# A hybrid attention and recurrence layer: values stationary in the heads, probabilities turned by a product with a diagonal of reciprocals, the branch's gate turned by VectorE and DMAs

## What is computed

```python
qh = _rms(heads(q)) * q_norm_w
kh = _rms(heads(k)) * k_norm_w
vh = heads(v)
log_f = log_sigmoid(f_logit + b_f)          # F = cumsum(log_f) over the sequence
# per head: s[t, u] = q_t . k_u / sqrt(128) + F_t - F_u for u <= t, p = softmax(s), att = p @ v
att = _forgetting_attention(qh, kh, vh, log_f)
y_a = att * silu(z_a)
y_a = einsum('bsw,wd->bsd', y_a, w_br_attn)
```

## Time and profile before

| | us |
|---|---|
| median of 3 runs | 2555.03 |
| lowest, highest | 2553.88, 2555.07 |
| the profiled execution's own time | 2555.0 |
| its span in the trace | 2553.2 |
| TensorE busy | 2522.7 (99%) |
| VectorE busy | 2013.0 (79%) |
| ScalarE busy | 1445.9 (57%) |
| GpSimd busy | 319.3 (13%) |

### The profile page before, as it was taken

The page is one execution under the profiler, slowest core; times in us unless marked ns, Lnnn a source line. Parts: engine busy times, 40 slices in busy tenths (PEclk is TensorE's granted clock), DMA queues, the critical chain, the costliest instruction groups (busy, mean ns, idle before and its releaser), DMA issues.

```text
span 2553.2 us, 31860 instructions
## 1 busy us (share of the span) xinstructions
PE 2522.7 (99%) x11399; PEld 2092.8 (82%) x11399; DVE 2013.0 (79%) x2163; ACT 1445.9 (57%) x1719; POOL 319.3 (13%) x577
## 2 busy tenths in 40 slices
PE   6999999999999999999999999999999999999999
PEld 5888888888888888888888888888888888888887
DVE  6999999999887666775777777668787878788885
ACT  6787666655555465655666666543434443555553
POOL 0000000000000000224556655200000000000000
PEclk9999999999999999999999999999999999999999
DMA  9999999999999666557777777789998989676675
GB/s 351 361 330 344 354 362 355 381 364 351 367 347 298 175 195 187 162 159 200 208 210 211 208 210 214 205 309 371 344 348 311 349 312 349 221 229 200 199 230 165
DMA packets 389617, 705.11 MB, mean 276 GB/s; under 512 B 36194, under 2 KB 99924, under 8 KB 388948
## 3 DMA queue, kind: packets, MB, share of 16 engines
q1 hardware_dynamic: 370656, 695.05, 81.5%
q0 software_dynamic: 18288, 7.90, 1.6%
q10 hardware_dynamic: 516, 0.13, 0.0%
HBM read 694.55 MB, written 7.88 MB: 275 GB/s over the span
## 4 chain that ended last, share of the span: by engine, by line
PE 96%; DMA 1%; SPq 1%; DVE 1%; ACT 0%; issue 0%; DVEq 0%; ACTq 0%
PE ps_acc L1650 27%; PE ps_acc L1585 25%; PE ps_acc L1587 25%; PE ps_t L1585 3%; PE ps_t L1587 3%; PE ps_t L1650 3%; PE ps_acc L1601 2%; PE ps_acc L1603 2%; SPq L624 1%; PE ps_acc L1642 0%; PE ps_acc L1644 0%; PE ps_acc L1643 0%; DMA land<-in_w_out 0%; DMA land<-in_w_gate 0%; PE ps_t L1725 0%; PE ps_t L1642 0%
## 5 line engine op out<-in xcount | busy, mean ns | idle before, releaser
L739 ACT ACTIVATE w_hi<-land 128x1024 fp32r<-128x1024 f32 x860 | 909.7, 1059 | 935.9 <-PE ps_acc L1587 588.0
L1019 DVE TENSOR_TENSOR w_lo<-land,w_hi 128x1024 fp32r<-128x1024 f32 x860 | 1049.8, 1222 | 399.9 <-ACT w_hi L739 394.1
L1585 PE MATMUL ps_acc<-w_hi,h_hi 128*128 128x512 f32 x2324 | 907.3, 390 | 0.5 <-ACT w_hi L739 0.5
L1587 PE MATMUL ps_acc<-w_hi,h_lo 128*128 128x512 f32 x2324 | 904.7, 389 | 0.0
L1650 PE MATMUL ps_acc<-w_lo,h_hi 128*128 128x512 f32 x2564 | 685.7, 389 | 1.1 <-DVE w_lo L1019 1.1
L1650 PEld LDWEIGHTS ps_acc<-w_lo,h_hi 128*128 128x128 f32 x2564 | 481.1, 188 | 101.9 <-DVE w_lo L1019 2.1
L1585 PEld LDWEIGHTS ps_acc<-w_hi,h_hi 128*128 128x128 f32 x2324 | 436.3, 188 | 91.6 <-ACT w_hi L739 1.3
L1587 PEld LDWEIGHTS ps_acc<-w_hi,h_lo 128*128 128x128 f32 x2324 | 436.5, 188 | 89.5
L1028 DVE SCALAR_TENSOR_TENSOR acc<-ada_ring,cvec,acc 128x1024 f32<-128x1024 f32 (+1 forms) x291 | 300.5, 1033 | 17.6 <-DMA ada_ring<-in_w_ada 10.9
L603 POOL DMA_DIRECT2D store<-xz x512 | 272.4, 542 | 198.1 <-DVE xz L1372 158.9
L1428 DVE SCALAR_TENSOR_TENSOR racc<-res_land,cvec,racc 128x1024 f32<-128x1024 f32 x124 | 158.7, 1280 | 0.9 <-DMA res_land<-in_w_ada 0.9
(11 more groups left out here) (304 smaller groups left out, 2339.2 us busy)
## 6 DMA issues: line engine op xcount, KB each, us to landing
land<-in_w_in SPq DMA_DIRECT2D x384, 512.0 KB, 5.5
land<-in_w_gate SPq DMA_DIRECT2D x256, 512.0 KB, 4.8
ada_ring<-in_w_ada SPq DMA_DIRECT2D x160, 512.0 KB, 6.2
res_land<-in_w_ada SPq DMA_DIRECT2D x128, 512.0 KB, 7.7
land<-in_w_out SPq DMA_DIRECT2D x92, 512.0 KB, 4.5
ada_ring<-in_w_ada SPq DMA_DIRECT2D x140, 256.0 KB, 5.0
land<-in_w_br_attn SPq DMA_DIRECT2D x64, 512.0 KB, 4.6
land<-in_w_br_rnn SPq DMA_DIRECT2D x64, 512.0 KB, 5.9
```

The costliest lines, as they stand in the source:

```text
L739: act.activation(w_hi[:, n % PARTS], land[:, n % LAND], ACT.Copy).then_inc(hi_rdy, 1)
L1019: dve.tensor_tensor(w_lo[:, n % PARTS], land[:, n % LAND], w_hi[:, n % PARTS].bitcast(F32), ALU.subtract).then_inc(split_done, 1)
L1585: pe.matmul(sums[:, t], l_hi(kk, t), w_hi[:, n % PARTS, kk], start=first and kk == 0 and not added, stop=False, skip_group_check=added)
L1587: ins = pe.matmul(sums[:, t], l_lo(kk, t), w_hi[:, n % PARTS, kk], start=False, stop=False, skip_group_check=added)
```

## The change

Four things change together.

1. The value step has v stationary and `prt` moving, so its result `ps_o` has channels on partitions as the next projection wants it. The step "y" on TensorE, its two transposes and its PSUM tile go; ScalarE rounds and VectorE splits straight from `yt` in SBUF.
2. The softmax's reciprocals are then needed along the free dimension. VectorE makes, per head, two diagonal matrices `diag` from `ident` and the reciprocals (`head_scale`), right behind the exponentials in the same slot, and TensorE's `probs` step is three full products of `pr` with `diag` in place of three transposes: it turns and scales at once.
3. The gate `z_a` must be multiplied in channels on partitions, too. `turn_za`, behind units 315, 319, ... 343 on VectorE, turns two heads at a time into the single buffer `za_turned`; GpSimd issues 16 DMAs per turning (128 in all) that write it back to `store`, between its `f_diff` of head 0 and of head 1. Each `turn_za` after the first waits until the DMAs of the one before have landed (`za_in`). Head 0's `prt` waits for all of them.
4. The order of steps within a slot: ScalarE has "y" ahead of "score", VectorE has "score", "y", "value" and then `head_scale`.

```diff
-PE_ORDER = ("score", "value", "y", "probs", "turn")
-ACT_ORDER = ("turn", "probs", "score", "y")
-DVE_ORDER = ("score", "probs", "value", "y")
+PE_ORDER = ("score", "value", "probs", "turn")
+ACT_ORDER = ("turn", "probs", "y", "score")
+DVE_ORDER = ("score", "y", "value")
...
+ZA_AT = {N_F + 28 + 4 * g: g for g in range(HEADS // 2)}
...
+        za_turned = at("za_turned", [P, BPJ, 2, NT, 32], F32, r_scr + 6 * K)
+        diag = [at(f"diag{h}", [P, NT, P], F32, blk(K_BLK + h)) for h in range(HEADS)]
...
             for h in range(HEADS):
+                if h == 1:
+                    for g in range(HEADS // 2):
+                        pool.wait_ge(za_t, g + 1)
+                        for i in range(BPJ):
+                            for jj in range(BPJ):
+                                pool.dma_start(store[32 * jj:32 * jj + 32, ZA_BLK + 2 * g:ZA_BLK + 2 * g + 2, :,
+                                                     32 * i:32 * i + 32].rearrange("p b t d -> p (b t) d"),
+                                               za_turned[32 * i:32 * i + 32, jj].rearrange("p b t d -> p (b t) d")
+                                               ).then_inc(za_in, 16)
                 pool.wait_ge(f_row_in[h % 2], h // 2 * 16 + 16)
...
+                    else:
+                        act.wait_ge(za_in, HEADS // 2 * 16 * BPJ * BPJ)
                     act.activation(prt[:], ps_p, ACT.Copy).then_inc(prt_rdy, 1)
                 if step == "y":
-                    act.wait_ge(y_t, h + 1)
-                    if h < HEADS - 1:
-                        act.wait_ge(y_rdy, 2 * h + 4)
-                    act.activation(ya_hi[:, h], ps_y, ACT.Copy).then_inc(ya_h, 1)
+                    act.wait_ge(y_rdy, h + 1)
+                    act.activation(ya_hi[:, h], yt[:], ACT.Copy).then_inc(ya_h, 1)
...
-                if step == "probs":
-                    dve.wait_ge(pr_rdy, 2 * h + 2)
-                    dve.reciprocal(rden[:, h % 2], den[:, h % 2]).then_inc(rden_rdy, 1)
                 if step == "value":
-                    dve.wait_ge(rden_rdy, h + 1)
                     dve.wait_ge(valued, h + 1)
                     if h:
-                        dve.wait_ge(y_t, h)
-                    for t in range(NT):
-                        dve.scalar_tensor_tensor(yt[:, t], ps_o[:, t], rden[:, h % 2, t:t + 1], store[:, ZA_BLK + h, t],
-                                                 ALU.mult, ALU.mult).then_inc(y_rdy, 1)
+                        dve.wait_ge(ya_rdy, h)
+                    dve.wait_ge(za_in, HEADS // 2 * 16 * BPJ * BPJ)
+                    dve.tensor_tensor(yt[:], ps_o, store[:, ZA_BLK + h], ALU.mult).then_inc(y_rdy, 1)
...
+            def head_scale(h):
+                dve.wait_ge(pr_rdy, 2 * h + 2)
+                st.did(dve.reciprocal(rden[:, h % 2], den[:, h % 2]))
+                st.sync()
+                for t in range(NT):
+                    dve.tensor_scalar(diag[h][:, t], ident[:], rden[:, h % 2, t:t + 1], None, ALU.mult
+                                      ).then_inc(diag_rdy, 1)
+
+            def turn_za(g):
+                dve.wait_ge(f_kept, 16)
+                dve.wait_ge(acc_free, FREED[FINAL["za", 3]][1])
+                if g:
+                    dve.wait_ge(za_in, g * 16 * BPJ * BPJ)
+                for i in range(2):
+                    ins = dve.transpose(za_turned[:, :, i].rearrange("p j t b -> p t j b"),
+                                        store[:, ZA_BLK + 2 * g + i].rearrange("p t (j a) -> p t j a", j=BPJ))
+                    if i == 0:
+                        st.did(ins)
+                ins.then_inc(za_t, 1)
...
+                if "score" in HEADS_AT.get(n - 2, {}):
+                    head_scale(HEADS_AT[n - 2]["score"])
+                if n in ZA_AT:
+                    turn_za(ZA_AT[n])
...
-                    for k in range(3):
-                        ins = pe.transpose(ps_p[:, k], pr[:, k], ident[:])
+                    pe.wait_ge(diag_rdy, NT * (h + 1))
+                    for k, t in enumerate((0, 1, 1)):
+                        ins = pe.matmul(ps_p[:, k], pr[:, k], diag[h][:, t], start=True, stop=True)
                     ins.then_inc(pr_t, 1)
...
-                    pe.matmul(ps_o[:, 0], prt[:, 0], store[:, V_BLK + h, 0], start=True, stop=True)
-                    pe.matmul(ps_o[:, 1], prt[:, 1], store[:, V_BLK + h, 0], start=True, stop=False)
-                    pe.matmul(ps_o[:, 1], prt[:, 2], store[:, V_BLK + h, 1], start=False, stop=True
+                    pe.matmul(ps_o[:, 0], store[:, V_BLK + h, 0], prt[:, 0], start=True, stop=True)
+                    pe.matmul(ps_o[:, 1], store[:, V_BLK + h, 0], prt[:, 1], start=True, stop=False)
+                    pe.matmul(ps_o[:, 1], store[:, V_BLK + h, 1], prt[:, 2], start=False, stop=True
                               ).then_inc(valued, 1)
-                if step == "y":
-                    pe.wait_ge(y_rdy, h * 2 + 2)
-                    if h:
-                        pe.wait_ge(ya_rdy, h)
-                    for t in range(NT):
-                        ins = pe.transpose(ps_y[:, t], yt[:, t], ident[:])
-                    ins.then_inc(y_t, 1)
```

More of the change, by code:

```diff
@@ L308 @@
 assert RG_START[-1] + RG_EVERY + 10 <= N_R + 5
+ZA_AT = {N_F + 28 + 4 * g: g for g in range(HEADS // 2)}
+assert N_F + 28 + 4 * (HEADS // 2 - 1) < N_HEAD
 MT_AT = {N_O - RU + 1 + 2 * k: k for k in range(CH)}
@@ L483, in build @@
         ps_o = ps_d[:, 0:2 * P].rearrange("p (a b) -> p a b", a=2)
-        ps_y = ps_d[:, 2 * P:4 * P].rearrange("p (a b) -> p a b", a=2)
         seq = lambda b: store[:, b].rearrange("p t d -> p (t d)")
@@ L522, in build @@
                                                  sem("pr_t"), sem("prt_rdy"))
-        valued, rden_rdy, y_rdy, y_t, ya_h, ya_rdy = (sem("valued"), sem("rden_rdy"), sem("y_rdy"), sem("y_t"), sem("ya_h"),
-                                            sem("ya_rdy"))
+        valued, diag_rdy, y_rdy, ya_h, ya_rdy = sem("valued"), sem("diag_rdy"), sem("y_rdy"), sem("ya_h"), sem("ya_rdy")
+        za_t, za_in = sem("za_t"), sem("za_in")
         bias_in, gate_rdy, gate_used = sem("bias_in"), sem("gate_rdy"), sem("gate_used")
@@ L1349, in head_step @@
                     dve.tensor_reduce(mx[:, 1:2], ps_s[:, 1:3], AX.XY, ALU.max, negate=True).then_inc(mx_rdy, 1)
-                if step == "probs":
-                    dve.wait_ge(pr_rdy, 2 * h + 2)
-                    dve.reciprocal(rden[:, h % 2], den[:, h % 2]).then_inc(rden_rdy, 1)
                 if step == "value":
-                    dve.wait_ge(rden_rdy, h + 1)
                     dve.wait_ge(valued, h + 1)
                     if h:
-                        dve.wait_ge(y_t, h)
-                    for t in range(NT):
-                        dve.scalar_tensor_tensor(yt[:, t], ps_o[:, t], rden[:, h % 2, t:t + 1], store[:, ZA_BLK + h, t],
-                                                 ALU.mult, ALU.mult).then_inc(y_rdy, 1)
+                        dve.wait_ge(ya_rdy, h)
+                    dve.wait_ge(za_in, HEADS // 2 * 16 * BPJ * BPJ)
+                    dve.tensor_tensor(yt[:], ps_o, store[:, ZA_BLK + h], ALU.mult).then_inc(y_rdy, 1)
                 if step == "y":
                     dve.wait_ge(ya_h, h + 1)
-                    dve.tensor_tensor(ya_lo[:, h], ps_y, ya_hi[:, h].bitcast(F32), ALU.subtract
-                                      ).then_inc(ya_rdy, 1)
+                    dve.tensor_tensor(ya_lo[:, h], yt[:], ya_hi[:, h].bitcast(F32), ALU.subtract).then_inc(ya_rdy, 1)
+            def head_scale(h):
[16 more added lines that the diff above has]
+                ins.then_inc(za_t, 1)
             def rg_step(off, n):
@@ L1736, in head_step @@
                     pe.wait_ge(prt_rdy, h + 1)
-                    if h >= 2:
-                        pe.wait_ge(ya_rdy, h - 1)
                     if h:
-                        pe.wait_ge(y_rdy, h * 2)
+                        pe.wait_ge(y_rdy, h)
                     else:
                         pe.wait_ge(acc_free, FREED[FINAL["v", 3]][1])
-                    pe.matmul(ps_o[:, 0], prt[:, 0], store[:, V_BLK + h, 0], start=True, stop=True)
-                    pe.matmul(ps_o[:, 1], prt[:, 1], store[:, V_BLK + h, 0], start=True, stop=False)
-                    pe.matmul(ps_o[:, 1], prt[:, 2], store[:, V_BLK + h, 1], start=False, stop=True
+                    pe.matmul(ps_o[:, 0], store[:, V_BLK + h, 0], prt[:, 0], start=True, stop=True)
+                    pe.matmul(ps_o[:, 1], store[:, V_BLK + h, 0], prt[:, 1], start=True, stop=False)
+                    pe.matmul(ps_o[:, 1], store[:, V_BLK + h, 1], prt[:, 2], start=False, stop=True
                               ).then_inc(valued, 1)
-                if step == "y":
-                    pe.wait_ge(y_rdy, h * 2 + 2)
-                    if h:
-                        pe.wait_ge(ya_rdy, h)
-                    for t in range(NT):
-                        ins = pe.transpose(ps_y[:, t], yt[:, t], ident[:])
```

(1 more changed line is left out.)

## The result

The changed kernel takes 2567.18 us (median of 4 runs, 2566.84 to 2568.67) against 2555.05 us; the ratio is 1.005 with a 95% interval of 1.0035 to 1.0064. It is 12.1 us slower. The forecast had the sign and the place, and more than twice the size: +27 us.

A forecast was written before the change was run, and what follows sets the result against it. TensorE was taken to bound the kernel, busy 2522.7 of 2553.2 us. 2555.0 + 2.1 (products) + 0 (heads on VectorE and ScalarE) + 24.5 (turning loop) = 2581.6, forecast 2582 us; range 2561 to 2608 us.

The forecast's parts named there:

- Bound and beat: TensorE bounds the kernel, busy 86.00 of 86 us at the turnings and 140.00 of 140 in the heads; 2.72 us a unit.
- Products on TensorE: In each head slot, `diag` products replace transposes of `pr` and `yt`: +0.13 us per head, +2.1 us for 16 heads.
- Heads on VectorE and ScalarE: In the head slots, VectorE gains 0.1 to 0.4 us, hidden from TensorE: 0 us, bounds -0.4 and +5 us.
- the bound: VectorE's two new 128-column scalings of `ident` in each head: between 0.175 and 0.338 us.
- The loop: Gate turnings, units 315 to 344: seven rounds take 104.0 us against 79.5 of room; TensorE waits 24.5 us.
- c: Step between GpSimd's DMA issues in a turning, 128 pieces each: 0.69 us, the middle of 0.60 and 0.77.
- The landing: Time from a turning's DMA issue to its landing, a term of each round: 3.2 us (median; 1.8 to 5.1).
- rival A: Gate turnings: an issue costs the same for 128 pieces as for 64; wait 7.7 us, 2565 us; chance 0.24.
- B: Gate turnings: the issue follows the long record, 0.93 us; wait 51.4 us, 2608 us; chance 0.08.
- C: Gate turnings: the round of 11.06 us fits into TensorE's four units, TensorE never waits; 2557 us; chance 0.08.
- D: TensorE loses clock in the gaps between turnings; 3 to 5 us more behind the last one, 2587 us; chance 0.05.

## Why the prediction went as it did

**Bound and beat: right.** TensorE was busy throughout in this stretch before, and every wait that reached it showed in the time.

**Products on TensorE: right.** +2.1 us forecast, 1.95 us measured by the beat.

**Heads on VectorE and ScalarE: right in effect.** No wait for `w_lo` grew. The wait for the exponentials is there, 4.0 us in 4 times, and the one for `ya_hi` went from 11.0 us in 15 times to 2.5 us in 5: one took the other's place. VectorE's two scalings are dearer than the bound said (below), and still hidden.

**The loop: right in its form, wrong in its terms.** The law (TensorE loses what seven rounds take beyond 79.5 us) came true twice, 12.1 us against 11.9 us measured (13.1 us a round), and 58.6 against 58.1 (19.7 us a round). The step that failed is the value of c. The forecast took 0.69 us between the price by starts (0.60) and by records (0.77); it was 0.54. That is 16 x 7 x 0.15 = 16.8 us too much. Both readings went by the count of pieces, and neither the records of DMAs that overlap nor that count is what an issue costs. The rule of the Trainium skill that I set beside it (page "DMA: Bandwidth & Descriptors", section "Anatomy of one DMA — SWDGE (gpsimd) path": many descriptors before their cost shows) was the better guide here: 0.55 us with 128 pieces on 32 partitions, 0.65 with 512.

**The landing: the second term, missed the other way.** 3.2 us, the median of single DMAs, stood for the landing of the last of 16. Round less the rest, 13.1 - 0.77 - 0.32 - 8.14 - 0.05, leaves 3.8 us. With the small terms that is 4.4 us too little in seven rounds. 24.5 - 16.8 + 4.4 = 12.1 us. The two errors went opposite ways; with the issue right and the landing as forecast, the sum would have been rival A's 7.7 us. Rival A had 2565 us; with this landing it is 2555.0 + 2.1 + 12.1 = 2569.2, and less the 1.5 us near unit 601 and 0.5 us at the start 2567.2, where the profiled run has 2566.8. VectorE's seven waits, forecast at 6 to 8 us each, are shorter for the same reason: 31.1 us in all, 4.4 us each.

**Rivals.** A had the mechanism and got a quarter of the chance, because I held the one other form of DMA in the trace for evidence of a slope when it differed in three things at once. B is out, c doesn't follow the long record. C would have needed rounds under 11.36 us; the shortest was 12.5. D did not happen with the gaps of the changed kernel, and did with the longer ones of the kernel with 32 DMAs, at about the price forecast (2.9 us against 3 to 5).

**Still open.** In the last turning GpSimd stands for 2.8 us between two issues for nothing that the profile shows, and for 2.8 to 5.0 us, once in each, in the other kernels with the turning (3.1 us ahead of the 129th issue with 32 DMAs). It lengthens a landing that the heads can wait for. In the five of them with 16 DMAs for two heads it stands behind the 113th issue each time, whether that is at 993 or at 1008 us, and in the kernel before as in the changed one GpSimd starts the fifth, tenth and fifteenth round of its 512 issues 2.0 us late. So it goes with a place in GpSimd's stream and not with the time. I found no cause.

## What to carry to other kernels

A chain that goes through several engines and comes back to the first costs its full round when one buffer serves it: compare the round with the bottleneck's period, not each engine's busy time with its room. Every term is multiplied by the number of rounds, so the step between issues and the landing of the last DMA, under the load of that stage, are worth a probe before anything else. A second buffer removes the loop, but look who owns its bytes next. And before a scaling is put into a product, see whether it is a factor per partition one step earlier.

## What the hardware showed beside that

In 11 of the 16 slots of the changed kernel the first of two equal `diag` scalings takes 0.75 to 0.85 us and the second 0.28. VectorE's and GpSimd's timelines of one slot, and of the next one:

```profile
1070.99 1.05 DVE L1378 TENSOR_SCALAR diag<-ident,rden 128x128 f32<-128x128 f32 x2
...
1079.16 0.48 DVE L1378 TENSOR_SCALAR diag<-ident,rden 128x128 f32<-128x128 f32 x2
```
```profile
1071.02 0.74 POOL L609 TENSOR_TENSOR f_diff<-f_diff,mask 128x256 f32<-128x256 f32 x1
...
1077.68 0.74 POOL L609 TENSOR_TENSOR f_diff<-f_diff,mask 128x256 f32<-128x256 f32 x1
```

The pair takes 1.05 us when GpSimd's operation on two SBUF tiles lies over it, and 0.48 us when that is over before. The second scaling follows when GpSimd's operation has ended (1071.76 us). The split of the weights is held up in the same way: the one that starts 0.01 us behind such an operation takes 1.81 us in place of 1.23.

```profile
905.63 1.81 DVE L1032 TENSOR_TENSOR w_lo<-land,w_hi 128x1024 fp32r<-128x1024 f32 x1 [0.99 <-ACT w_hi L752]
```
```profile
905.62 0.73 POOL L609 TENSOR_TENSOR f_diff<-f_diff,mask 128x256 f32<-128x256 f32 x1
```

VectorE's operations that take an input from PSUM, the maxima (0.29 and 0.41 us) and the product for `yt` (0.42 us), keep their time beside GpSimd's. The Trainium skill, page "SBUF — State Buffer", section "🔬 SBUF: two separate sides", has VectorE and GpSimd take a shared pair of ports for a whole instruction; this trace agrees for the scaling and for the split. The same page has GpSimd's DMA issues blocked while VectorE runs an operation in one of its two-port modes. Beside splits and block transposes they kept their 0.54 us, and no `diag` scaling ran beside one, so no run here tests that.
